# Scoring the four maps of two differential heads together, in four row groups, at the end of a step

## The reference, cut to what matters

```python
s = jnp.einsum('bqhmd,bkhmd->bhmqk', qb, k).astype(jnp.float32) * scale   # h: 4 heads, m: 2 maps, d: 32
s = jnp.where(kpos[None, :] <= qpos[:, None], s, NEG)
p = jax.nn.softmax(s, axis=-1)
a = p[:, :, 0] - lam * p[:, :, 1]
return jnp.einsum('bhqk,bkhd->bqhd', a.astype(v.dtype), v)
```

## Time and profile before

| | |
|---|---|
| median of 3 runs | 3546.88 us (3545.88 to 3547.21) |
| profiled execution | 3541.27 us, its span 3539.3 us |
| PE busy | 3464.1 us, 98% of the span |
| DVE, ACT, POOL busy | 47%, 42%, 44% |
| chain that ended last | PE 65%, issue 22%, POOL 8%, DVE 3%, ACT 1% |
| attention, layer 0 and layer 1 | about 540 to 700 us and 1605 to 1768 us |
| granted TensorE clock | full for nearly the whole span |

### The profile page before, as it was taken

One profiled execution on the slowest core, in us unless ns is written; L12 is line 12 of the kernel. 1 busy time (PEld: TensorE's weight loads), 2 busy tenths in 40 slices (PEclk: granted clock), 3 DMA queues, 4 the chain that ended last, 5 costly groups with the idle time before them and its releaser, 6 DMA issues.

```text
span 3539.3 us, 56010 instructions
## 1 busy us (share of the span) xinstructions
PE 3464.1 (98%) x21291; PEld 2903.6 (82%) x21291; DVE 1663.5 (47%) x2762; ACT 1476.7 (42%) x2450; POOL 1550.2 (44%) x1384
## 2 busy tenths in 40 slices
PE   8999999999999999999999999999999999999998
PEld 7999776689998999776589997888888785778887
DVE  8456634574658556644575656111112504651112
ACT  5344535553546344535554544212112335443223
POOL 4555545445545554545445544232323542034443
PEclk9999999999999999999999999999999999999999
DMA  4343444223433343444223333222222323023332
GB/s 125 106 113 85 105 131 126 90 77 103 118 87 93 100 115 85 108 126 133 90 72 107 107 90 96 66 60 65 59 61 58 90 59 101 19 61 100 96 95 65
DMA packets 569569, 322.57 MB, mean 91 GB/s; under 512 B 30282, under 2 KB 563376, under 8 KB 569008
## 3 DMA queue, kind: packets, MB, share of 16 engines
q1 hardware_dynamic: 569392, 320.22, 31.7%
HBM read 318.08 MB, written 2.10 MB: 90 GB/s over the span
## 4 chain that ended last, share of the span: by engine, by line
PE 65%; issue 22%; POOL 8%; DVE 3%; ACT 1%; POOLq 0%; ACTq 0%; DVEq 0%
PE psum L3100 21%; PE psum L2993 16%; PE psum L3207 12%; POOL w_lo L985 7%; PE psum L3413 2%; PE psum L3490 2%; PE psum L3447 1%; PE psum L3387 1%; PE psum L3134 1%; PE psum L3515 1%; PE psum L3137 1%; PE psum L3254 1%; PE psum L3532 1%; PE psum L3415 1%; POOL set_lo L1040 0%
## 5 line engine op out<-in xcount | busy, mean ns | idle before, releaser
L985 POOL TENSOR_TENSOR w_lo<-w_raw,w_hi 128x512 fp32r<-128x512 f32 x488 | 656.1, 1367 | 1109.2 <-ACT w_hi L1077 1109.2
L1077 ACT ACTIVATE w_hi<-w_raw 128x1024 fp32r<-128x1024 f32 x244 | 257.6, 1058 | 843.1 <-PE psum L2993 710.2
L2993 PE MATMUL psum<-h_hi,w_hi 128*128 128x512 f32 x1136 | 454.5, 400 | 1.5 <-POOL w_lo L985 1.5
L2993 PE MATMUL psum<-h_hi,w_lo 128*128 128x512 f32 x1136 | 447.2, 394 | 0.0
L2993 PE MATMUL psum<-h_lo,w_hi 128*128 128x512 f32 x1136 | 444.3, 391 | 0.0
L1040 POOL TENSOR_TENSOR set_lo<-w_raw,set_hi 128x512 fp32r<-128x512 f32 x224 | 292.5, 1333 | 223.3 <-ACT set_hi L1156 220.3
L3100 PE MATMUL psum<-t_hi,set_hi 128*128 128x256 f32 x1280 | 363.6, 284 | 9.9 <-ACT gated L1146 8.0
L3100 PE MATMUL psum<-t_lo,set_hi 128*128 128x256 f32 x1280 | 362.7, 283 | 0.0
L3100 PE MATMUL psum<-t_hi,set_lo 128*128 128x256 f32 x1280 | 362.7, 283 | 0.0
L3207 PE MATMUL psum<-a_hi,set_hi 128*128 128x512 f32 x704 | 277.0, 393 | 2.8 <-DVE a_lo L2142 2.8
L3207 PE MATMUL psum<-a_lo,set_hi 128*128 128x512 f32 x704 | 274.2, 389 | 0.0
(11 more groups left out here) (628 smaller groups left out, 8019.4 us busy)
## 6 DMA issues: line engine op xcount, KB each, us to landing
w_raw<-ffn_w SPq DMA_DIRECT2D x120, 512.0 KB, 3.8
w_raw<-ffn_w_gate SPq DMA_DIRECT2D x88, 512.0 KB, 4.1
w_raw<-ffn_w_up SPq DMA_DIRECT2D x88, 512.0 KB, 4.0
ada_raw<-ada_w SPq DMA_DIRECT2D x72, 512.0 KB, 4.7
w_raw<-ffn_w_down SPq DMA_DIRECT2D x64, 512.0 KB, 3.8
w_raw<-w_in SPq DMA_DIRECT2D x60, 512.0 KB, 3.9
w_raw<-ffn_w_down SPq DMA_DIRECT2D x32, 384.0 KB, 3.2
w_raw<-w_out SPq DMA_DIRECT2D x24, 512.0 KB, 3.6
```

Source lines behind the costliest of these rows:

```text
L985: last = nc.gpsimd.tensor_tensor(w_lo[:, i, at], w_raw[:, i, at], w_hi[:, i, at].bitcast(F32), ALU.subtract)
L1077: nc.scalar.activation(w_hi[:, pos, :], w_raw[:, pos, :], ACT.Copy).then_inc(hi_ready, 1)
L2993: last = nc.tensor.matmul(dst, w[:, pos, k * P:(k + 1) * P], rhs[g][r](k0 + k), start=k == 0 and m == 0, stop=k == nk - 1 and m == 2)
```

## The change

Steps 2 and 4 of each tile become joint steps (`JOINT`). There TensorE scores two units at once, units 2 and 3 at step 2 and units 4 and 5 at step 4: first four score matmuls, one after another in four row groups and four banks, then four mask matmuls, with one signal per unit. The joint scores stand at the end of the step, behind its transposes and value products (but ahead of the modulation sums), and wait until the exponentials of both units before have been read. Steps 3 and 5 score nothing. On DVE the maximum of units 2 and 4 moves behind the step's copy, reciprocal and `mod` addition; those of units 3 and 5 stay at the start of their steps. ACT and POOL keep their streams.

```diff
+JOINT = (2, 4)
...
+                def maximum(t):
+                    b = score_banks(t)
+                    dve.wait_ge(*unit_scores_done(layer, t))
+                    nc.vector.tensor_reduce(neg_max[:, 2 * t:2 * t + 2], psum[:, b:b + 2, 0:(TILE_AT[t // UN] + 1) * P], AX_X, ALU.max,
+                                            negate=True).then_inc(max_ready.sem, 1)
...
-                    if t < NU:
-                        b = score_banks(t)
-                        dve.wait_ge(*unit_scores_done(layer, t))
-                        nc.vector.tensor_reduce(neg_max[:, 2 * t:2 * t + 2], psum[:, b:b + 2, 0:(TILE_AT[i] + 1) * P], AX_X, ALU.max,
-                                                negate=True).then_inc(max_ready.sem, 1)
+                    if t < NU and step not in JOINT:
+                        maximum(t)
...
                     if t < NU:
                         at = slice(TILE_AT[i] * P, (TILE_AT[i] + 1) * P)
+                        if step in JOINT:
+                            maximum(t)
                         if step == AT_CMP_TURN:
...
+                def scores(first, count):
+                    if first + count > 2:
+
+                        pe.wait_ge(*exp_ready(layer, first + count - 2))
+                    tile = TILE_AT[first // UN]
+                    n = (tile + 1) * P
+                    for u in range(first, first + count):
+                        for m, head in enumerate(UNIT_MAPS[u % UN]):
+                            q, k, _ = key_values(*head)
+                            nc.tensor.matmul(psum[:, score_banks(u) + m, 0:n], q(slice(tile * P, (tile + 1) * P)), k(n), start=True, stop=False)
+                    for u in range(first, first + count):
+                        for m in range(2):
+                            last = nc.tensor.matmul(psum[:, score_banks(u) + m, n - P:n], ident_b[:], causal_b[:], start=False, stop=True)
+                        last.then_inc(scores_done.sem, 1)
...
-                        if t >= 2:
-
-                            pe.wait_ge(*exp_ready(layer, t - 1))
...
+                        if step not in JOINT and step - 1 not in JOINT:
+                            scores(t, 1)
...
                         last.then_inc(o_done.sem, 1)
+                    if t < NU and step in JOINT:
+                        scores(t, 2)
```

More of the change, by code:

```diff
@@ L99 @@
 FIRST_NSA_EVENT = EVENT_OF[FIRST_NSA]
+JOINT = (2, 4)
+assert all(UNIT_MAPS[s + m][0] == ("diff", s - 2 + m, 0) for s in JOINT for m in range(2))
 def event_of(u):
```

## The result

The changed kernel takes 3580.89 us (median of 4 runs, 3577.13 to 3583.2), the kernel before 3547.05: a ratio of 1.0105, 95% interval [1.0092, 1.0119], thus 34 us more where 20 were forecast. The direction was right; the time lies 0.9 us outside the range. The profiled execution of the changed kernel is the slowest of its four (3583.2 us, span 3581.2), that of the kernel before (3541.27) is faster than any of its timed runs, so that the two spans differ by 41.9 us, 8 more than the medians. The trace can only be asked about these 41.9: 19.9 us arise in the first layer's attention, 16.1 in the second's (where the kernel before has 10.2 us of half clock of its own, in the first 3.4), 1.5 in a short stretch at half clock some 87 us behind each, and the rest in pieces outside of them.

The account below looks back on a forecast made before the run. TensorE, busy for 98% of the span, was taken as the bound. 3541.3 (profiled) + 17.2 of waits + 3 of clock = 3561.5; with the median 5.6 above the profiled run, 3567 us, range 3550 to 3580.

Parts of the forecast that it names:

- What bounds the stage, and the ring: In the attentions TensorE bounds; scores, maximum, exponentials and the next scores form a ring, tight at two places of a tile.
- 8 to 11 us longer in each layer: Sign to look for in the changed kernel's profile: each layer's attention this much longer, all else alike.
- Four row groups at once: Joint scores: four groups take what one pair takes, saving 1.06 us per joint step (512 tile), 11.8 in two layers.
- First place: Joint scores of units 2 and 3, 384 tile: L3447 0.9 us late, TensorE idle ahead of it about 3.5 us.
- Second place: Joint scores of units 4 and 5, 384 tile: unit 7, waiting for exponentials 5, scored 3.0 us late.
- The sum of a layer: Waits in the four tiles of one layer's attention: 2.2 + 0.9 + 3.0 + 2.5 = 8.6 us, both layers 17.2.
- The clock: New holes in the tiles bring three more half-clock stretches over the eight tiles: 3 us.
- the clock gives way in every tile: Rival: eight more, longer half-clock stretches (1.5 us each), 17.2 + 12 gives 3576; 14%.
- The range: Whole time: 17.2 off by perhaps a third and 0 to 8 us of clock, 3556 to 3574, widened to 3550 to 3580.

Follow-up runs that it names:

- e8: The changed kernel with filling matmuls in both holes, at the end of step 3 and at step 5: 3563.69 us, ratio 1.0057.
- e2: The changed kernel, but each joint step scores its two units one after another: 3575.77 us, ratio 1.0092.
- e7: e6, and DVE takes the maxima of both units of a joint group one after the other: 3561.76 us, ratio 1.0052.
- e6: The changed kernel, but at step 4 ACT and DVE split the previous tile's last outputs before exponentials and maximum of unit 4: 3565.77 us, ratio 1.0064.
- e5: The changed kernel measured again, unaltered, as a yardstick: 3578.65 us, ratio 1.0096.
- e11: e7 with filling matmuls at the end of step 3 and at step 5: 3546.4 us, ratio 1.0014.

## Why the prediction was right in kind and too small

The step that failed is the term of the sum for the clock: 3 us were taken, and it cost 15. Beside it the forecast of the waits missed one link, TensorE's modulation behind the low part.

- *What bounds the stage, and the ring.* Right. TensorE's wait of the earlier trace rows grew from 0.57 to 3.28 us, the ring of the second joint group got longer, and 36.0 of the 41.9 us lie in the two attentions. The sign "8 to 11 us longer in each layer" was not met (19.9 and 16.1); only e8, at full clock, has it (9.8 in layer 0).
- *Four row groups at once.* Right: 0.87 us to the masks in the 384 tile. e2 shows that this saving lies inside waits, as the forecast had it for the first place.
- *First place.* Right: L3447 0.98 us late (0.9 forecast), its wait 3.28 (about 3.5). e7 shows the cause named, the queue behind `cmp_sums`: with maximum 3 ahead of it L3447 is late by 0.12 only and its wait falls by 0.9. What is left of the wait, 2.4 us against 0.57 before, is mostly the place of the scores of units 3 and 4 (0.97 us each with their masks), as the forecast had it.
- *Second place.* Right in place and roughly in size, wrong in its last link. The forecast let unit 7 wait for "maximum 5 0.96 and exponentials 5 1.23". In fact TensorE's modulation sums of step 5 wait for the low part already, to use bank 7, and units 6 and 7 are queued behind them. The forecast follows DVE's and ACT's streams but never looked at what TensorE has queued ahead of unit 7 with a wait of its own. At full clock (e8) the loss is 3.5 instead of 3.0 us in the 384 tile and 3.4 instead of 2.5 in the 256 tile; unit 7 comes 0.6 and 0.75 us behind the end of exponentials 5. At half clock, in the changed kernel's 384 tile, it is 2.8 us. e6 takes this link away. The sum of a layer is 9.8 instead of 8.6, nearer 11 with the 128 tile at equal clock.
- *The clock.* This is the term that was mis-sized, and it carries most of the error. "Between none and one in each of the eight tiles more I take three: 3 us". Measured: 34.1 us at 0.50 in layer 0's attention, against 3.4 before, and one stretch of 17.1 us where 3.42 was taken for the unit. They cost 10.2 us in layer 0 (after - e8). In whole times e5 - e8 is 15 us. So of some 36 us of e5's loss about 21 are waits (17.2 forecast) and 15 clock (3 forecast). The split is not exact: by e8's interval its 21 us stand for 14 to 26, and the filling also removes half clock that the kernel before has, so the waits are if anything a little more. The forecast counted holes and priced one stretch each. But at half clock TensorE's own pieces in the ring double (joint scores 1.60 instead of 0.87, modulation 1.87 instead of 1.0), the ring gets longer, TensorE idles in it again, and the clock stays down over several stretches in a row. That the longer pieces bring the next stretch is read from the order of the rows; no run changes them alone. The rival "the clock gives way in every tile", at 12 us and 3576, was nearer than the forecast in mechanism and size; the changed kernel's profile has half clock in seven of the eight tiles.
- *The range.* The forecast allowed 0 to 8 us for the clock, which took 15, and a third of 17.2 for the waits. That the time lies only 0.9 us outside is owed to the widening to 3580 for other cases, not to the clock term. Waits and clock were taken as independent errors; but the clock falls behind the waits, so both err the same way.

The Trainium skill (TensorE: Matmul & The Clock Gate, HAM oscillation) describes a loop whose idle stretches throttle the clock again and again. This trace agrees in kind: 17.1 us at 0.50 behind 3.66 us in which TensorE worked for 1.07.

## What to carry to other kernels

Packing matmuls saves TensorE time, and that is worth something only where TensorE is the limit. Look first at what the packed group must wait for and at what then waits for it. Then go through the waiting engine's stream for every instruction between, each with its own waits. Two units scored at once take all four score banks, so the next scores wait for maxima and exponentials that used to run beside other scores, and the engines that read the scores must have their queues ordered for the second unit, too. And price a hole in TensorE's work with the half clock that it brings, which here came to some two thirds of the price of the waits themselves.

## What the runs showed of the hardware

- Four fp32 score matmuls of 32 rows in four row groups and banks take as long as two: 1.07 us to the masks at 512 columns (557.84 to 558.91), 0.87 at 384.

```profile
557.84 1.14 PE L3414 MATMUL psum<-k_diff,q_diff 32*128 32x512 f32 x8
558.91 0.40 PE L3417 MATMUL psum<-causal_b,ident_b 128*128 128x128 bf16 x4
```

- The four groups at half clock, in the 384 tile, take 1.60 us to the masks (641.94 to 643.54) where they take 0.87 at full clock.
- Useless bf16 matmuls of 0.06 us each (58 in 3.41 us) in the holes keep the clock up: 15 us less in the median of e8 against e5, and of e11 against e7, with no work saved.
- 34.1 us at half clock in layer 0's attention cost 10.2 us (changed kernel less e8), 0.30 us for each, since TensorE also waits in them; 3.4 us of it in the dense work behind the attention cost 1.5.
- Stretches at half clock behind the attention, in otherwise dense work, appear in the changed kernel some 87 us later (from 807.2 and 1892.6 us) and not in the kernel before. Each stands right behind a wait of 1.8 us, but the kernel before has the same wait at the same place in both layers and keeps the full clock. In the first layer, changed kernel and kernel before:

```profile
806.47 0.35 PE L3109 MATMUL psum<-t_hi,set_hi 128*128 128x256 f32 x1 [1.77 <-ACT gated L1150]
```

```profile
786.59 0.36 PE L3100 MATMUL psum<-t_hi,set_hi 128*128 128x256 f32 x1 [1.78 <-ACT gated L1146]
```

  So the same hole can cost a stretch or not; what decides it stays open.
